# Branch half of the output products moved from the output stage into the delta-rule tiles

## The reference

```
def _mix_out(p, o, ...):
    y_gdn = _gdn_out(o, p[..., Z_OFF:A_OFF], gdn_norm)       # scan channels, 0 to 511
    y_f = _fnet(p[..., F_OFF:C_OFF])                          # branch channels
    y_c = _conv_module(p[..., C_OFF:IN_W], ...)               # branch channels
    return jnp.concatenate([y_gdn, y_f, y_c], axis=-1) @ w_out

# _gdn_chunked: per chunk of 64 tokens and head
decay = exp(where(incl, g[..., :, None] - g[..., None, :], NEG))
a_mat = where(strict, einsum("bhnid,bhnjd->bhnij", kb, k) * decay, 0.0)
sol = triangular_solve(a_mat + eye(CHUNK), rhs, lower=True, unit_diagonal=True)
u, w = sol[..., :dv], sol[..., dv:]
# ... then a scan over the chunks with u, w, q and k

# _layer
x = x + gt1 * mix(p, o, rows)
x = x + gt2 * peer(_rms(x, norm2) * (1 + sc2) + sh2)
if not last:
    xc = xc + cgt1 * mix(pc, oc, None)
    xc = xc + cgt2 * peer(...)
```

## Time and profile before

| what | us |
|---|---|
| runs | 4374.01, 4365.52, 4371.61 |
| median of the runs | 4371.61 |
| the profiled execution: its span, the only time given for it | 4365.4 |
| tiles, layer 0 (345.4 to 501.0) | 155.6 |
| scan, layer 0 (501.0 to 555.5) | 54.5 |
| output stage, layer 0 (555.5 to 673.2) | 117.7 |
| tiles, layer 1 (2765.5 to 2919.0) | 153.5 |
| scan, layer 1 (2919.0 to 2970.0) | 51.0 |
| output stage, layer 1 (2970.0 to 3063.0) | 93.0 |

### The profile page before, as it was taken

The page is one execution under the profiler, slowest core; times in us unless marked ns, Lnnn a source line. Parts: engine busy times, 40 slices in busy tenths (PEclk is TensorE's granted clock), DMA queues, the critical chain, the costliest instruction groups (busy, mean ns, idle before and its releaser), DMA issues. The chain is left out here.

```text
span 4365.4 us, 55131 instructions
## 1 busy us (share of the span) xinstructions
PE 3693.1 (85%) x18945; PEld 1903.6 (44%) x18945; DVE 3006.0 (69%) x6251; ACT 1720.2 (39%) x5270; POOL 1645.7 (38%) x1508
## 2 busy tenths in 40 slices
PE   7998998988888887888886888888898888888777
PEld 3566854533433433433432335775443343343222
DVE  3964666975775875875875885557797687687444
ACT  2223623444344344344342454353444433433333
POOL 0004513443443443444443432352444444444332
PEclk9999999999999999999998999899999999999999
DMA  8360159999999999999999997015999999999997
GB/s 336 122 239 29 37 198 367 416 421 421 418 415 422 414 417 421 407 420 422 410 412 369 408 394 303 2 37 190 404 422 421 421 421 421 421 413 421 422 421 325
DMA packets 238985, 1506.07 MB, mean 345 GB/s; under 512 B 28433, under 2 KB 33617, under 8 KB 71153
## 3 DMA queue, kind: packets, MB, share of 16 engines
q0 software_dynamic: 184320, 1342.26, 74.7%
q1 hardware_dynamic: 54384, 160.28, 9.9%
HBM read 1490.32 MB, written 12.12 MB: 344 GB/s over the span
## 5 line engine op out<-in xcount | busy, mean ns | idle before, releaser
L2831 PE MATMUL ps<-low,pediag 128*128 128x512 f32 x2180 | 1058.7, 615 | 226.1 <-ACT pediag L2741 219.3
L2606 DVE CUSTOM_DVE_ANT_0 low<-low,hc 128x1024 f32<-128x1024 f32 x545 | 667.8, 1225 | 359.3 <-DMA low<-in_experts_dram,eid 342.0
L2585 POOL DMA_INDIRECT low<-in_experts_dram,eid x539 | 595.0, 1104 | 812.4 <-PE ps L2831 783.2
L2733 ACT ACTIVATE low<-peact 128x1 f32<-128x1 f32 x1152 | 232.1, 201 | 1335.0 <-DVE peact L2606 1334.0
L2831 PEld LDWEIGHTS ps<-low,pediag 128*128 128x128 f32 x2180 | 388.9, 192 | 824.5 <-ACT pediag L2741 499.4
L2741 ACT ACTIVATE pediag<-cst,low 128x128 f32<-128x128 f32 x1152 | 462.5, 402 | 42.1 <-PE ps L2831 4.5
L2831 PE MATMUL ps<-wide_a,pediag 128*128 128x512 f32 x640 | 307.8, 612 | 54.4 <-ACT pediag L2741 54.2
L2736 ACT ACTIVATE low<-low,gw 128x1 f32<-128x1 f32 x1152 | 339.1, 294 | 37.4
L2831 PE MATMUL ps<-wide_b,pediag 128*128 128x512 f32 x640 | 303.3, 605 | 50.7 <-ACT pediag L2741 48.5
L2060 PEld LDWEIGHTS ps<-qkvT,arena 128*128 128x128 f32 x2560 | 312.0, 193 | 75.4 <-issue 75.4
L2060 PE MATMUL ps<-qkvT,arena 128*128 128x128 f32 x2560 | 313.1, 276 | 2.4 <-ACT qkvT L2024 2.4
(11 more groups left out here) (497 smaller groups left out, 5773.9 us busy)
## 6 DMA issues: line engine op xcount, KB each, us to landing
pjdot<-in_mod_t_dram SPq DMA_DIRECT2D x64, 512.0 KB, 5.2
arena<-in_w_mod_dram SPq DMA_DIRECT2D x24, 1024.0 KB, 14.4
arena<-in_peer_wq_dram SPq DMA_DIRECT2D x8, 2048.0 KB, 17.1
low<-in_experts_dram,eid POOLq DMA_INDIRECT x609, 8.7
pjw<-in_w_cols_dram SPq DMA_DIRECT2D x18, 512.0 KB, 3.7
plw<-in_w_cols_dram SPq DMA_DIRECT2D x18, 512.0 KB, 8.1
x_rows<-low SPq DMA_DIRECT2D x10, 512.0 KB, 7.7
qkvT<-mod_rows SPq DMA_DIRECT2D x9, 512.0 KB, 7.6
```

The source lines that it names most:

```text
L2585: nc.gpsimd.indirect_dma_start(ring.row(g), None, table, bass.IndirectOffsetOnAxis(eid[:, j % 2, k:k + 1], 0)).then_inc(ring.landed(g), 16)
L2606: nc.vector.tensor_tensor_reduce(out=dot_out if final else ring.row(g)[:, 0:D], in0=ring.row(g)[:, 0:D], in1=hc[:, j % 2, :], scale=1.0, s ...
L2733: nc.scalar.activation(ge[:, g % 2, 0:1], act_v[:, j % 2, k:k + 1], ACT.Gelu_apprx_tanh).then_inc(gelu_ready, 1)
L2831: last = nc.tensor.matmul(ps[:, half, :], diag[:, g % DIAGS, :], ring.row(g)[:, D + half * 512:D + (half + 1) * 512], start=k == 0, stop=k ...
```

## The change

The four branch matmuls of each half no longer stand in the output stage. A new class, BranchRows, works them on PE inside gdn_tiles: a table gives how many matmuls follow each of the five levels and the turned inverse in every tile (1, 1, 2, 2, 1, 1 in layer 0: two halves a tile; 1 each in layer 1, until all 32 are done). They accumulate in one PSUM bank, number 2, which the gram had (the gram goes to bank 3, the sums of the gates from 3 to 7, and the turned inverse, which also uses 3, waits for the gram's readers). DVE multiplies a finished half by the gate and adds it to a row of x behind its other work of a level. SP gets a program in this stage: it loads the branch half of w_out (2 MB), the gate and, one after the other, the rows of x, and stores each row to x_rows in DRAM when both its halves are added.

The output stage multiplies the scan channels alone, four matmuls to a half, into oT and with the scan half of w_out loaded during the scan; it reads x from x_rows. Its PE order begins with two turns and then two products. The wide buffers now hold the weights, gate, x row and temporaries in the tiles, and the scan's state; X lies in two places, one for even and one for odd tiles. The ring takes its rows in another order, since other rows are free early: besides the row outside the ring, three rows (2, 3, 6) in layer 0 and the rows 2 and 3 among others in layer 1 need wait for no product. An outer group of semaphores goes around gdn_tiles.

```
+EARLY_LEVELS = ((1, 1, 2, 2, 1, 1), (1, 1, 1, 1, 1, 1))
...
+class BranchRows:
+    BANK = 2
...
+    def issued(self, t, n):
+        return min(t * sum(self.share) + sum(self.share[:n + 1]), self.halves * KD // 2)
...
+    def sp(self, sp):
+        n = len(self.tiles)
+        sp.dma_start(self.w, self.kit.w_out[self.L, H * P:D, :].rearrange("(k p) n -> p k n", p=P)).then_inc(self.w_in, 16)
+        self.load_gate(sp, 0)
+        self.load(sp, 0)
+        for i in range(n):
+            sp.wait_ge(self.added, 2 * (i + 1))
+            sp.dma_start(self.rows(i), self.xb).then_inc(self.saved, 16)
+            if i + 1 in self.turns:
+                self.load_gate(sp, i + 1)
+            sp.wait_ge(self.saved, 16 * (i + 1))
+            if i + 1 < n:
+                self.load(sp, i + 1)
+    def pe(self, pe, t, n):
+        for m in range(self.products, self.issued(t, n)):
+            q, k = divmod(m, KD // 2)
+            i, half = divmod(q, 2)
+            if m == 0:
+                pe.wait_ge(self.w_in, 16)
+            if k == 0 and q:
+                pe.wait_ge(self.gated, q)
+            last = self.nc.tensor.matmul(self.kit.ps[:, self.BANK, :], self.mixT[:, H + k, self.tiles[i], :],
+                                         self.w[:, k, half * 512:(half + 1) * 512], start=k == 0, stop=k == KD // 2 - 1)
+            if k == KD // 2 - 1:
+                last.then_inc(self.prod, 1)
+        self.products = self.issued(t, n)
+    def dve(self, dve, t, n):
+        done = self.issued(t, n - 1) if n else self.issued(t - 1, len(self.share) - 1) if t else 0
+        self.add(dve, done // (KD // 2))
+    def rest(self, dve):
+        self.add(dve, self.halves)
+    def add(self, dve, upto):
+        for q in range(self.sums, upto):
+            i, half = divmod(q, 2)
+            cols = slice(half * 512, (half + 1) * 512)
+            dve.wait_ge(self.gate_in, 16 + 16 * sum(i >= n for n in self.turns))
+            dve.wait_ge(self.prod, q + 1)
+            if q:
+                dve.wait_ge(self.added, q)
+            self.nc.vector.tensor_tensor(self.yb, self.kit.ps[:, self.BANK, :], self.gate[:, cols], ALU.mult
+                                         ).then_inc(self.gated, 1)
+            dve.wait_ge(self.gated, q + 1)
+            dve.wait_ge(self.x_in, 16 * (i + 1))
+            self.nc.vector.tensor_tensor(self.xb[:, cols], self.xb[:, cols], self.yb, ALU.add
+                                         ).then_inc(self.added, 1)
+        self.sums = max(self.sums, upto)
...
+                early.sp(sp)
...
-                                last = nc.tensor.matmul(small(2, i)[R, h, :], key, with_key, start=True, stop=True)
+                                last = nc.tensor.matmul(small(3, i)[R, h, :], key, with_key, start=True, stop=True)
...
+                    pe.wait_ge(gram_used, t + 1)
...
+                        early.pe(pe, t, n)
                     if t + 1 < NT:
                         turn_inverse(t + 1)
+                    early.pe(pe, t, NL)
...
+                        early.dve(dve, t, n)
...
+                early.rest(dve)
...
-            if row < 4:
+            if row < 2:
                 return HALVES
-            if row > 7:
-                return 1
-            here = [i for i in range(n_tiles) if tiles[i] // 2 == row - 4]
-            return 2 * (max(here) + 1) if here else 1
+            here = [i for i in range(n_tiles) if i // 4 == row - 4]
+            return 2 * (max(here) + 1) if here else 0
...
-            rows = kit.x_d[t * P:(t + 1) * P, :]
-            if L == 0:
-                rows = kit.ctx[0, t * P:(t + 1) * P, :] if t < NC else kit.x[0, (t - NC) * P:(t - NC + 1) * P, :]
-            sp.dma_start(xb[:, b, :], rows).then_inc(x_in[b], 16)
+            sp.dma_start(xb[:, b, :], kit.x_d[t * P:(t + 1) * P, :]).then_inc(x_in[b], 16)
...
-                sp.dma_start(w[1], w_out_half(kit, L, 1)).then_inc(w_in, 16)
...
-                def branch_part(q):
+                def product(q):
 
                     i, half = divmod(q, 2)
-                    t = tiles[i]
-                    if q == 1:
-                        pe.wait_ge(w_in, 16)
+                    cols = slice(half * 512, (half + 1) * 512)
+                    pe.wait_ge(copied, n_tiles if q >= 4 else i + 1)
                     if gated_for(q):
                         pe.wait_ge(gated, gated_for(q))
-                    if q >= 4:
-                        pe.wait_ge(copied, n_tiles)
-                    for k in range(H, KD):
-                        nc.tensor.matmul(ps[:, bank_of(q), :], mixT[:, k, t, :], w[half][:, k, :],
-                                         start=k == H, stop=False)
-
-                def scan_part(q):
-
-                    i, half = divmod(q, 2)
-                    t = tiles[i]
-                    pe.wait_ge(copied, i + 1)
                     for k in range(H):
-                        last = nc.tensor.matmul(ps[:, bank_of(q), :], mixT[:, k, t, :], w[half][:, k, :],
-                                                start=False, stop=k == H - 1)
+                        last = nc.tensor.matmul(ps[:, bank_of(q), :], oT[:, i, k, :], w[:, k, cols],
+                                                start=k == 0, stop=k == H - 1)
                     last.then_inc(prod_ready, 1)
 
-                def product(q):
-                    branch_part(q)
-                    scan_part(q)
-
-                branch_part(0)
                 turn(0)
-                scan_part(0)
                 turn(1)
+                product(0)
+                product(1)
                 turn(2)
-                product(1)
                 turn(3)
                 product(2)
...
-HELD_ROWS = [5, 6, 2, 3, 4]
+HELD_ROWS = [2, 3, 6, 4, 5]
...
+                with phase(nc, kit, *EARLY_SEMS) as sems:
+                    early = BranchRows(nc, kit, L, tiles, mixT, w1[:, :], w0, sems)
+                    gdn_tiles(nc, kit, L, first, hT, qkvT, gate, kt, us, wT, qkd, decs, dts, early)
+                gdn_scan(nc, kit, L, first, qkvT, kt, us, wT, qkd, decs, dts, o, scan_half(w0), w1[:, :])
...
-                ring = RowRing(first_row, rows, [5, 6, 2, 3, 4, 0, 1, 7], sems[0:RING + 1])
...
+                ring = RowRing(first_row, rows, [2, 3, 6, 4, 5, 0, 1, 7], sems[0:RING + 1])
```

More of the change, by code:

```diff
@@ L1423, in step_of, with __init__, rows, load @@
     return next(s for s in range(T // CHUNK) if place(s, d)[0:2] == (t, half))
-def gdn_tiles(nc, kit, L, first, hT, qkvT, gate, kt, us, wT, qkd, decs, dts):
+EARLY_LEVELS = ((1, 1, 2, 2, 1, 1), (1, 1, 1, 1, 1, 1))
+EARLY_SEMS = ["ew_in", "ex_in", "egate_in", "eprod", "egated", "eadded", "esaved"]
+class BranchRows:
+    BANK = 2
+    def __init__(self, nc, kit, L, tiles, mixT, w, room, sems):
+        self.nc, self.kit, self.L, self.tiles, self.mixT = nc, kit, L, tiles, mixT
+        self.w = w.rearrange("p (k n) -> p k n", n=D)
+        self.xb, self.gate, self.spare = room[:, 0:D], room[:, D:2 * D], room[:, 2 * D:4 * D]
+        self.yb = kit.hc[:, 1, 0:512]
+        self.w_in, self.x_in, self.gate_in, self.prod, self.gated, self.added, self.saved = sems
+        self.turns = [i for i in range(1, len(tiles)) if (tiles[i] >= NC) != (tiles[i - 1] >= NC)]
+        self.halves, self.share = 2 * len(tiles), EARLY_LEVELS[L]
+        self.products = self.sums = 0
+    def issued(self, t, n):
+        return min(t * sum(self.share) + sum(self.share[:n + 1]), self.halves * KD // 2)
+    def rows(self, i):
+        t = self.tiles[i]
+        return self.kit.x_d[t * P:(t + 1) * P, :]
+    def load(self, sp, i):
+        t, rows = self.tiles[i], self.rows(i)
+        if self.L == 0:
+            rows = self.kit.ctx[0, t * P:(t + 1) * P, :] if t < NC else self.kit.x[0, (t - NC) * P:(t - NC + 1) * P, :]
+        sp.dma_start(self.xb, rows).then_inc(self.x_in, 16)
+    def load_gate(self, sp, i):
+        sp.dma_start(self.gate, mod_row(self.kit, self.L, int(self.tiles[i] >= NC), 2)).then_inc(self.gate_in, 16)
+    def sp(self, sp):
[44 more added lines that the diff above has]
+        self.sums = max(self.sums, upto)
@@ L1430, in gdn_tiles @@
+def gdn_tiles(nc, kit, L, first, hT, qkvT, gate, kt, us, wT, qkd, decs, dts, early):
     G = 2 * H
@@ L1446, in gdn_tiles @@
         ra, rb, blk, w = blocks(0, 2), blocks(2, 3)[:, 0], blocks(3, 5), blocks(5, 6)[:, 0]
-        X = sb("X", [P, 2, 2, 2, H, C])
+        X = [room.rearrange("p (d k h n) -> p d k h n", d=2, k=2, h=H) for room in (kit.arena[:, 5 * NT * GW:5 * NT * GW + D], sb("X", [P, D]))]
         vt = kit.hc[:, 0, :].rearrange("p (a h n) -> p a h n", a=2, h=H)
-        ru = sb("ru", [P, 2, H, P])
-        rw = sb("rw", [P, 2, H, P])
-        sums_sb = sb("sums", [P, 2, 4, NT * H])
-        dect = sb("dect", [P, 2, NT * H])
-        bg = sb("bg", [P, 2, NT, H])
-        beta = sb("beta", [P, 2, NT, G])
+        ru, rw = (early.spare[:, i * D:(i + 1) * D].rearrange("p (d h n) -> p d h n", d=2, h=H) for i in range(2))
+        NG = 2 * NT * H
```

(33 more changed lines are left out.)

63 lines of the change are left out of this document (32 added, 31 removed).

## The result

| kernel | median us | runs | lowest to highest |
|---|---|---|---|
| before | 4371.61 | 5 | 4365.52 to 4374.24 |
| changed | 4445.5 | 5 | 4443.56 to 4448.48 |

A forecast was written before the change was run, and what follows sets the result against it. TensorE was taken to bound the tiles, rows of x the output stage's end. Layer 0 +46 +7 -10.5, layer 1 +27 -5.5, barriers +2: +66 on 4365.4, 4431, set to 4434 us; range 4416 to 4452, widened to 4394 to 4460.

The forecast's parts named there:

- PE's order in the tiles is full: Tile stage: PE busy 20.72 of 23.30 us a step, so moved matmuls lengthen layer 0's steady step to 30.7 us.
- The rival that PE's busy time overstates its load: Tiles: 128x512 matmuls slip between 64x64 ones, tile stage grows 9 us by tail and barriers; 4349 to 4358; chance 0.05.
- The price of a matmul: Each moved 128x512 matmul costs PE 0.857 us: 41.1 us for layer 0's 48, 27.4 for layer 1's 32.
- the gaps of the earlier trace: PE's idle gaps of 1.19, 0.30 and 0.45 us in a steady step, all that moved matmuls can have for nothing.
- layer 0's miss: Layer 0's tiles to the scan's first DMA: +54 us forecast, +61.5 measured.
- The bank wait: Behind level 3 in layer 0, PE waits 2.3 us a tile until DVE's multiply frees the one PSUM bank.
- The tail: End of layer 0's tiles: last half's multiply and add (1.4), then its row's store (5.3), delay the scan 7 us.
- Layer 1's tiles: One matmul a level: 27.4 us of matmuls, less 9.5 covered by gaps, plus 9.5 of bank waits: +27 us.
- The output stages: Give back 10.5 us in layer 0, where rows of x end the last waits, and 5.5 in layer 1.
- The experts: Expert stages, at a DMA share of 1.01, keep their length; freeing ring rows sooner is worth nothing.
- The adds on DVE: Layer 0's tiles: two 0.69 us instructions for each of 12 halves, 16.6 us, lie in DVE's idle 9.7 us a step.

The follow-up runs named there:

- e9: Changed kernel with early matmuls in two groups of four (behind level 2 and the turned inverse), each half's four run twice: 4483.18 us, steps 35.9 us.
- e3: Changed kernel with only the first of each early half's four matmuls done, all waits, multiplies, adds, loads and stores kept: 4405.7 us (one run).
- e6: Changed kernel without early matmuls, their multiplies and adds, an 8-column instruction standing for each add: 4356.34 us.
- e1: Changed kernel with early matmuls placed 1, 1, 2, 0, 2, 2 in both layers, so a half begins only at level 4: 4415.32 us.
- e2b: Changed kernel with 32 idle 64x64 matmuls run where PE waits for the bank (level 3 in layer 0, level 4 in layer 1): 4439.31 us.
- e5: Changed kernel with DVE's multiply and add of a finished half moved straight behind a level's X updates: 4425.23 us.
- e4: Kernel before with the output stage's branch matmuls left out, nothing else changed: 4345.61 us (one run).
- e8: Changed kernel with early matmuls in two groups of four, behind level 0's gram and level 4's updates, in both layers: 4446.69 us (one run).

## Why the prediction was right, and where its sizes were off

- **PE's order in the tiles is full.** Right: e9 gives the full 0.857 us for each further matmul, e3 and e6 the way down. The rival that PE's busy time overstates its load fell with the result and with e9. The Trainium skill, "Perfetto Trace Analysis", section "Identifying the Most-Contended Engine", calls matmul busy time a poor measure of how near a kernel is to its roofline, since pipelined matmuls look smaller in the trace. Read so, it does not speak for the rival, as the prediction has it. How near these tiles are, no run measures; of the room in PE's order the busy time spoke true, 35.9 - 29.0 = 6.9 us for eight more.
- **The price of a matmul.** Mis-sized. 0.857 us is right within a group, but five of the six groups of a step add some 0.2 us each. The prediction also took the gaps of the earlier trace rows for all there are; the one of 0.37 us ahead of an update (445.72) closed too. Up to level 4's w products the surcharges, this gap and a bank that was free 0.2 sooner cancel, by luck: in the step from 403.53 level 3's and level 4's w products are 2.2 and 6.2 us late, as forecast. Behind them 1.9 us come on top, where 1.27 were forecast. So a step at full clock is 31.4, not 30.7: 0.7 x 4 = 2.8 us of layer 0's miss.
- **The bank wait**, forecast 2.3 us, measured 2.52 in layer 0, and behind the X updates and the first inverse, as said. In layer 1 the five waits were of 1.1 to 2.75 us, where about 2 each were forecast. e1, which has one bank too but lets it be emptied in time, is 30 us faster than the change; that holds the wait, the clock behind it and, in layer 1, fewer groups. The Trainium skill ("Perfetto Trace Analysis", section "Matmuls") says that independent matmul groups should rotate through different PSUM banks. No run here gives the halves a second bank, so what one is worth is not shown; e1 shows that the wait can go without it.
- **The clock.** The prediction has no term for it. PE stood still for 2.5 us, and behind four of five such waits in layer 0 the clock was at 0.50; e2b and e5, with that idle time filled or cut to 1.54, have none of it there. 33.0 + 32.7 + 32.8 - 3 x 31.4 = 4.3 us of layer 0's miss. With the 2.8 that makes 7.1 of the 7.5. The fourth fall comes after the last gram, where a tail shorter than forecast makes up for it, by luck.
- **The tail.** Forecast 7 and 1 for tail and barrier, measured 5.4 - 0.9 = 4.5 for both. Store and barriers took 3.65 us, where 5.3 were taken for the store alone from a place in the output stage at a DMA share of 0.77 (643.0 to 648.2 before); behind the changed kernel's tiles the share is 0.36 (559.5 to 563.1).
- **Layer 1's tiles**, alone 33.5 us longer, 28 forecast. Behind its waits of 2.52 and 2.75 us, which ended at 2913.78 and 2974.46, the clock stood at 0.50 too; at layer 0's 1.3 to 1.6 us each that would be some 3 of the 5.5. The lone matmuls' 0.2 us, less the gap of 0.37 in each step, would cover the rest. Neither was tested by itself.
- **The output stages.** Right in size and mechanism: the last add ends 97.3 us behind the stage's start, forecast 97.6 (653.1 - 555.5), and a row of x stands ahead of it. e4, with no branch products at all, gives back only 1.5 us more in the two stages.
- **The experts** neither lost nor gained, though more ring rows were free early.
- **The adds on DVE** were hidden where they stand in the change (besides the bank, PE waits 0.24 us at most in the steady tile from 403.53), but not everywhere, as e8 shows.

## What to carry to other kernels

Work moved to a stage where its engine is the bound was paid for in full here, and gave back only the time by which it was the bound where it stood: 80 matmuls at 0.857 us are 68.5, some 87 with group starts, bank wait and clock; against it stand 13, what the output stages give back less tail and barriers. Read the giving stage by what its last waits end on, not by the engine's busy time. An accumulation put in between other work wants its bank emptied by the time it begins again; that took a change of one table and was worth 30 of the 74 us, still not enough.

## What was not expected of the hardware

- Behind idle waits of 2.52 us TensorE's granted clock stood at 0.50 for about 3 us in four of five places of the changed kernel's layer 0; behind those of 1.54 us it stayed at 1.0 in all of them, in e5. One wait of 2.52 us had no such effect. Its length does not tell it apart: in e8 four of five waits of 2.52 us were followed by 0.50 and in e3 two of five, in e3's layer 1 a wait of 2.90 us (ended at 2901.26) was not, and in e2b's a wait of 2.14 us (ended at 2872.87) was. What does is open.
- Idle matmuls that filled most of the wait made the kernel's tiles faster, by 6.5 us in layer 0 (e2b).
- A group of 128x512 matmuls between 64x64 ones costs about 0.2 us of PE's time beyond its matmuls: 1.06 us for one, 1.92 for two, 3.63 for four, where 0.857 each is the rate within a long row of them.
